# Four of eleven down tiles of each feed-forward as seven block products, moved behind the up tiles

## The reference

```python
def swiglu_ffn(x, w1, w2):
    a, b = jnp.split(x @ w1, 2, axis=-1)
    return (jax.nn.silu(a) * b) @ w2            # w1: 1024 x 5632, w2: 2816 x 1024

def conv_ffn(v, w_up, conv_w, conv_b, w_down):
    a, lin = jnp.split(v @ w_up, 2, axis=-1)
    a = sum(ap[:, j:j + s] * conv_w[j] for j in range(CONV_W)) + conv_b   # ap: a, padded; 3 taps
    return (jax.nn.gelu(a) * lin) @ w_down

# first block:   x = x + 0.5 * swiglu_ffn(rms_norm(x, g), w1, w2)    before and after the mixers
# second block:  x = x + conv_ffn(rms_norm(x, g), w_up, conv_w, conv_b, w_down)
```

## Time and profile before

| | us |
|---|---|
| median of 3 runs | 2239.8 (2239.71 to 2240.84) |
| the profiled execution | 2240.4 |
| its span, first to last instruction | 2238.7 |
| PE busy in the span | 2222.5 (99%) |
| DVE busy | 1529.8 (68%) |
| ACT busy | 1210.0 (54%) |
| DMA, bytes moved | 409.38 MB, mean 183 GB/s |

### The profile page before, as it was taken

How to read it: one execution, slowest core, us unless ns; L and a number is a source line. 1 busy time by engine, 2 the same in 40 slices (tenths; PEclk the granted TensorE clock), 3 DMA queues, 4 the chain that set the end, 5 groups by cost and what they waited for, 6 DMA issues and landing times.

```text
span 2238.7 us, 30449 instructions
## 1 busy us (share of the span) xinstructions
PE 2222.5 (99%) x12350; PEld 1898.8 (85%) x12350; DVE 1529.8 (68%) x2112; ACT 1210.0 (54%) x1812; POOL 67.6 (3%) x118
## 2 busy tenths in 40 slices
PE   8999999999999999999999999999999999999998
PEld 7888987888888889878888988888888988888887
DVE  6557578665665575786656866786777766786766
ACT  6456455454564564555545655455555555455554
POOL 0000000000000000000000200000000100000000
PEclk9999999999999999999999999999999999999999
DMA  8565544455545655434655544445555544445553
GB/s 286 192 232 184 199 180 151 171 188 188 188 186 190 232 186 204 182 144 169 232 189 190 187 151 165 156 153 181 190 192 178 189 151 165 156 166 181 188 188 113
DMA packets 62803, 409.38 MB, mean 183 GB/s; under 512 B 7976, under 2 KB 9512, under 8 KB 15304
## 3 DMA queue, kind: packets, MB, share of 16 engines
q1 hardware_dynamic: 62664, 407.44, 50.5%
HBM read 405.83 MB, written 2.10 MB: 182 GB/s over the span
## 4 chain that ended last, share of the span: by engine, by line
PE 94%; DVE 3%; ACT 1%; DMA 1%; issue 0%; SPq 0%; POOLq 0%; DVEq 0%; POOL 0%; ACTq 0%
PE bank L593 20%; PE bank L594 20%; PE bank L595 20%; PE bank L640 18%; PE bank L647 9%; DVE w_lo L270 1%; PE bank L393 1%; PE bank L1733 1%; PE bank L1745 1%; DMA w_raw<-in_tiles 0%; PE bank L2345 0%; PE bank L2052 0%; PE bank L2513 0%; PE bank L2062 0%; PE bank L2072 0%; PE bank L2532 0%
## 5 line engine op out<-in xcount | busy, mean ns | idle before, releaser
L270 DVE TENSOR_TENSOR w_lo<-w_raw,w_hi 128x2048 fp32r<-128x2048 f32 x367 | 835.1, 2284 | 69.0 <-ACT w_hi L240 68.6
L240 ACT ACTIVATE w_hi<-w_raw 128x2048 fp32r<-128x2048 f32 x359 | 685.3, 1912 | 107.7 <-DMA w_raw<-in_tiles 107.5
L640 PE MATMUL bank<-hT,w_hi 128*128 128x512 f32 x1920 | 459.5, 390 | 2.4 <-DVE w_lo L270 2.4
L640 PEld LDWEIGHTS bank<-hT,w_hi 128*128 128x128 f32 x1920 | 355.8, 188 | 73.8 <-DVE w_lo L270 2.8
L593 PE MATMUL bank<-w_hi,hT 128*128 128x512 f32 (+2 forms) x832 | 327.9, 394 | 0.3
L595 PE MATMUL bank<-w_hi,hT 128*128 128x512 f32 (+2 forms) x832 | 318.9, 383 | 0.0
L594 PE MATMUL bank<-w_lo,hT 128*128 128x512 f32 (+2 forms) x832 | 318.8, 383 | 0.0
L647 PEld LDWEIGHTS bank<-hT,w_lo 128*128 128x128 f32 x1920 | 247.7, 191 | 10.3
L647 PE MATMUL bank<-hT,w_lo 128*128 128x256 f32 x1920 | 250.9, 283 | 0.0
L593 PEld LDWEIGHTS bank<-w_hi,hT 128*128 128x128 f32 x832 | 156.8, 188 | 37.6 <-issue 7.9
L595 PEld LDWEIGHTS bank<-w_hi,hT 128*128 128x128 f32 x832 | 156.6, 188 | 31.3
(11 more groups left out here) (395 smaller groups left out, 2984.8 us busy)
## 6 DMA issues: line engine op xcount, KB each, us to landing
w_raw<-in_tiles SPq DMA_DIRECT2D x368, 1024.0 KB, 4.8
a_cmp_w<-in_cmp_w SPq DMA_DIRECT2D x2, 2048.0 KB, 7.8
shifted<-in_bias SPq DMA_DIRECT2D x12, 256.0 KB, 7.2
w_raw<-in_tiles SPq DMA_DIRECT2D x8, 256.0 KB, 5.7
a_gm_rows<-in_rows SPq DMA_DIRECT2D x2, 768.0 KB, 7.0
x_res<-in_x SPq DMA_DIRECT2D x2, 512.0 KB, 5.1
a_ret_rows<-in_rows SPq DMA_DIRECT2D x2, 512.0 KB, 8.0
b_rows<-in_rows SPq DMA_DIRECT2D x2, 512.0 KB, 6.2
```

The costliest lines, as they stand in the source:

```text
L240: act.activation(k.hi[slot][:], k.raw[slot][:], ACT.Copy).then_inc(k.hi_done[slot], 1)
L270: dve.tensor_tensor(k.lo[slot][:], k.raw[slot][:], k.hi[slot][:].bitcast(F32), ALU.subtract).then_inc(k.lo_done[slot], 1)
L640: pe.matmul(bank[:], k.hi[slot][:, w], k.hT[:, c].rearrange("p a s -> p (a s)"), start=c == 0, stop=False)
```

## The change

The feed-forwards' down tiles 2 to 8 move behind all up tiles. They then come in the order 2, 6, 3, 7, 4, 5, 8, before the two last, 9 and 10. Tiles 2, 3, 4, 5 (S) are multiplied by Strassen's algorithm in Winograd's form: the product of activations (2 x 2 blocks) and weights (2 x 2 blocks) takes seven block products in place of eight. DVE makes sums of weight blocks into a second, "made" tile that takes a ring slot of its own but is not loaded (`None` among the places); it is split into hi and lo as any other. DVE also makes four sums of activation blocks (`add_blocks`), which ACT and DVE split (`sums_hi`, `sums_lo`). Four of the products gather in banks 0 to 3, which the up tiles no longer need, and `recombine` adds them to x in eight steps. The activations of tiles 2 to 8 are kept in buffers of their own (`z_hi`, `z_lo`). Some semaphores are merged and some buffers moved to make room. A ring of 33 tiles becomes one of 37.

```diff
@@ class Ring
+    def make(self, dve, m, link):
+        k, slot, made = self.k, self.slot[m], self.slot[m + 1]
+        assert self.places[m + 1] is None and self.lo <= m
+        w = k.raw[slot][:].rearrange("p (c n e) -> p c n e", c=2, n=2)
+        t = k.raw[made][:].rearrange("p (q e) -> p q e", q=4)
+        dve.wait_ge(k.landed[slot], 16 * self.nth[m])
+        dve.wait_ge(k.used[made], self.before[m + 1])
+        link(dve.tensor_tensor(t[:, 0:2], w[:, :, 1], w[:, 0], ALU.subtract))
+        link(dve.tensor_tensor(t[:, 2], w[:, 1, 1], t[:, 0], ALU.subtract))
+        dve.tensor_tensor(t[:, 3], w[:, 1, 0], t[:, 2], ALU.subtract).then_inc(k.landed[made], 16)
...
+STRASSEN = (2, 3, 4, 5)
+LATER = (6, 7, 8)
+TAIL = (2, 6, 3, 7, 4, 5, 8)
+ENDING = (FFN_PAIRS - 2, FFN_PAIRS - 1)
+def ffn_order():
+    order = [("up", 0, 0), ("up", 0, 1)]
+    for i in range(1, FFN_PAIRS):
+        order += [("up", i, 0), ("up", i, 1)]
+        if i - 1 not in TAIL + ENDING:
+            order.append(("down", i - 1))
+    for i in TAIL + ENDING:
+        order.append(("down", i))
+        if i in STRASSEN:
+            order.append(("made", i))
+    return order
...
+    def strassen(self, pe, i):
...
+        ring.ready(pe, n)
+        product(self.acc[0][0], a12, n, 2, False, False)
+        product(self.acc[0][1], s4, n, 3, False, False)
+        if first:
+            for j in range(2):
+                pe.wait_ge(self.summed[j], self.parts(FFN_PAIRS - 1, 1))
+        product(k.bank[0], a11, n, 0, first, last).then_inc(k.used[ring.slot[n]], 1)
+        ring.ready(pe, n + 1)
+        product(self.acc[1][0], a22, n + 1, 3, False, False)
+        product(k.bank[1], s1, n + 1, 0, first, last)
+        product(k.bank[2], s2, n + 1, 2, first, last)
+        product(k.bank[3], s3, n + 1, 1, first, last).then_inc(k.used[ring.slot[n + 1]], 1)
@@ def tensor
-            if i < N - 1:
...
+            if i - 1 not in TAIL + ENDING:
+                self.whole(pe, i - 1)
+        pe.wait_ge(self.chain, self.links + 4 * len(STRASSEN))
+        for i in TAIL:
+            if i in STRASSEN:
+                self.strassen(pe, i)
+            else:
+                self.whole(pe, i)
@@ def scalar
                 self.split_hi(act, i, j)
+                if j == 0 and i - 1 in STRASSEN:
+                    self.sums_hi(act, i - 1)
             if i < FFN_PAIRS - 1:
                 k.ring.hi_to(act, self.up_at(i, 1) + SLOTS)
+        k.ring.hi_to(act, self.down_at(ENDING[0]) + 1)
+        k.ring.wait_used(act, self.down_at(STRASSEN[-1]) + 1, 1)
+        act.activation(self.flat(0), k.bank[0][:], ACT.Copy).then_inc(self.act_copy, 1)
+        k.ring.hi_to(act, self.end + 1)
@@ def vector
                 self.add_parts(dve, i, j, 1)
+                if j == 0 and i - 1 in STRASSEN:
+                    self.add_blocks(dve, i - 1, link)
                 self.combine(dve, i, j)
                 self.split_lo(dve, i, j)
+                if j == 1 and i - 1 in STRASSEN:
+                    self.sums_lo(dve, i - 1, link)
...
+            if i == FFN_PAIRS - 2:
+                ring.make(dve, self.down_at(STRASSEN[0]), link)
+            if i < FFN_PAIRS - 1:
                 ring.lo_to(dve, self.up_at(i, 1) + SLOTS - 1 + (self.conv is not None and i == 1))
+        for i in STRASSEN[1:]:
+            if i == STRASSEN[2]:
+                ring.lo_to(dve, self.down_at(i))
+            ring.make(dve, self.down_at(i), link)
+            ring.lo_to(dve, self.down_at(i) + 2)
+        ring.lo_to(dve, self.down_at(ENDING[0]) + 1)
+        self.recombine(dve, link)
+        ring.lo_to(dve, self.end)
...
+    def add_blocks(self, dve, i, link):
...
+        dve.tensor_tensor(s1, a21, a22, ALU.add)
+        link(dve.tensor_tensor(s3, a11, a21, ALU.subtract))
+        link(dve.tensor_tensor(s2, s1, a11, ALU.subtract))
+        link(dve.tensor_tensor(s4, a12, s2, ALU.subtract))
+    def sums_lo(self, dve, i, link):
+        n = STRASSEN.index(i)
+        dve.wait_ge(self.act_copy, self.act_copies + n + 1)
+        link(dve.tensor_tensor(self.z_lo[i][:, 3:7], self.sums[n % 2][:], self.z_hi[i][:, 3:7].bitcast(F32),
+                               ALU.subtract))
+    def recombine(self, dve, link):
...
+        k.ring.wait_used(dve, self.down_at(STRASSEN[-1]) + 1, 1)
+        dve.wait_ge(self.act_copy, self.act_copies + len(STRASSEN) + 1)
+        to_x(0, 0, p1)
+        link(dve.tensor_tensor(u, p6, u, ALU.add))
+        link(dve.tensor_tensor(v, p5, u, ALU.add))
+        to_x(0, 1, v)
+        link(dve.tensor_tensor(u, p7, u, ALU.add))
+        to_x(1, 0, u)
+        link(dve.tensor_tensor(v, p5, u, ALU.add))
+        link(to_x(1, 1, v))
```

More of the change, by code:

```diff
@@ L268, in lo_to @@
             slot = self.slot[m]
+            if m + 1 < len(self.places) and self.places[m + 1] is None:
+                dve.wait_ge(k.landed[self.slot[m + 1]], 16 * self.nth[m + 1])
             dve.wait_ge(k.hi_done[slot], self.nth[m])
@@ L648, in lo_part @@
     return last
-def ffn_places(base):
[L653 to L662, removed]
+STRASSEN = (2, 3, 4, 5)
[13 more added lines that the diff above has]
+    return order
+FFN_ORDER = ffn_order()
+FFN_AT = {tile: n for n, tile in enumerate(FFN_ORDER)}
+FFN_SIGNALS = [1 if tile[0] != "up" else 2 for tile in FFN_ORDER[:-1]] + [2]
+FFN_SIGNALS[0] = 1
+END_SIGNALS = FFN_SIGNALS[:-1] + [4]
+def ffn_places(base):
+    at = {"up": lambda i, j: base + 2 * i + j, "down": lambda i: base + 2 * FFN_PAIRS + i, "made": lambda i: None}
+    return [at[tile[0]](*tile[1:]) for tile in FFN_ORDER]
+LINKS = 6 * len(STRASSEN) + 5
 class Ffn:
@@ L752, in down, with activations, product @@
         return last
+    def activations(self, i, t, j):
+        if i in LATER:
+            return self.z_hi[i][:, 2 * j + t], self.z_lo[i][:, 2 * j + t]
+        ts = slice(t * P, (t + 1) * P)
+        return self.g_hi[i % 2][j][:, ts], self.g_lo[i % 2][j][:, ts]
+    def strassen(self, pe, i):
+        k, ring, n = self.k, self.k.ring, self.down_at(i)
+        a11, a12, a22, s1, s2, s3, s4 = range(7)
+        first, last = i == STRASSEN[0], i == STRASSEN[-1]
+        def product(bank, block, tile, q, start, stop):
+            w, slot = slice(q * 512, (q + 1) * 512), ring.slot[tile]
+            return three_passes(pe, bank[:], (self.z_hi[i][:, block], self.z_lo[i][:, block]),
+                                (k.hi[slot][:, w], k.lo[slot][:, w]), start, stop)
+        ring.ready(pe, n)
[10 more added lines that the diff above has]
+        product(k.bank[3], s3, n + 1, 1, first, last).then_inc(k.used[ring.slot[n + 1]], 1)
     def tensor(self, pe, following):
@@ L785, in tensor, with whole @@
                     last.then_inc(used(i), 1)
+    def whole(self, pe, i):
+        k = self.k
+        k.ring.ready(pe, self.down_at(i))
+        for j in range(2):
+            pe.wait_ge(self.glo_done[j], self.base + i + 1)
+            for t in range(NT):
+                last = self.down(pe, i, t, j)
+        last.then_inc(k.used[k.ring.slot[self.down_at(i)]], 1)
     def end_by_columns(self, pe, following):
@@ new lines, in vector @@
+        self.recombine(dve, link)
+        ring.lo_to(dve, self.end)
+        if self.block_end:
+            ring.lo_half(dve, self.end, 0)
+        else:
+            ring.lo_to(dve, self.end + 1)
+    def add_blocks(self, dve, i, link):
+        n = STRASSEN.index(i)
+        (a11, a21), (a12, a22) = ([g[:, t * P:(t + 1) * P] for t in range(NT)] for g in self.g)
+        s1, s2, s3, s4 = (self.sums[n % 2][:, q] for q in range(4))
+        for j in range(2):
+            dve.wait_ge(self.g_done[j], self.base + i + 1)
+        dve.tensor_tensor(s1, a21, a22, ALU.add)
+        link(dve.tensor_tensor(s3, a11, a21, ALU.subtract))
+        link(dve.tensor_tensor(s2, s1, a11, ALU.subtract))
+        link(dve.tensor_tensor(s4, a12, s2, ALU.subtract))
```

76 lines of the change are left out of this document (49 added, 27 removed).

## The result

The changed kernel takes 2328.85 us (median of four runs, 2326.01 to 2331.29), the kernel before beside it 2240.02 (2239.71 to 2240.84): a ratio of 1.0395, 95% interval 1.0383 to 1.0407, 88.8 us slower. The forecast was 2312 with a range of 2280 to 2335. The prediction was right in sign and range; the time lies 17 us above its value, 0.85 us above the upper end of the forecast itself (2300 to 2328), and in the stretch that the rival of the clock had (2316 to 2335). The profiled execution of the changed kernel spans 2329.5 us, that of before 2238.7.

The account below looks back on a forecast made before the run. PE, busy 99%, was taken as the bound, with VectorE's in-order list making it wait after the change. First block 16.7 us, second 57.0, about 1 off: +72.7, giving 2312 us; forecast 2300 to 2328, range 2280 to 2335.

Parts of the forecast that it names:

- the rival of the clock: Clock falls at new waits, above all the second block's 8 us one: +10 us, 2322; chance 0.10, most of it 2316-2335.
- PE's saving: A Strassen tile saves PE 0.68 us, a feed-forward with four of them 2.73, all six feed-forwards 16.4.
- VectorE's prices: VectorE's added work: making a tile 2.75 us, its split 2.20, block sums with low parts 1.95, recombining 5.45.
- Second block: Pairs of up tiles take VectorE 12.87 us, 14.8 with sums, against PE's 11.10; PE starts down tile 6 29.8 late.
- First block's turn: From up to down tiles, PE is 5.3 us late at tile 6: waits of 2.4 before a11, 2.9 before tile 6.
- Tile 10: End of the tail, both blocks: PE waits 1.4 us for its low part, 0.7 more once, ahead of the second block.
- The first block without the clock: First block's four feed-forwards together: 4 x (5.3 + 1.4 - 2.7) + 0.7 = 16.7 us slower.
- the prediction's own last sign: Forecast is wrong if PE's matmul steps of 0.43 us turn up behind the second block's long wait.
- the walk: Step-by-step count of VectorE's in-order list against PE's needs in all feed-forwards; it gave the forecast 2312 us, without the clock.
- The larger edit is the move: Moving tiles 2 to 8 behind the up tiles leaves VectorE 11.10 us per up pair, where it had 16.57.
- The rival in which the first block's turn costs nothing: Waits there are covered by slack in ACT or PE while the second block pays: +44 us, 2284; chance 0.12.
- The rival in which the saving stands: Second-block pairs pass through VectorE in 11.10 us or less, PE stays the bound: 2223.4 us; chance 0.06.

Follow-up runs that it names:

- order_fixed: The changed kernel with VectorE's list reordered at the turn in both blocks (first made tile earlier, down tile 6's low part before tile 3's making): 2303.69 us.
- zero_fill: The changed kernel with matmuls of a zero weight block put into PE's list where it waits in the tails: 2320.94 us.
- move_only: The changed kernel with the seven down tiles moved but all multiplied whole, without Strassen's work: 2259.2 us, ratio 1.0084 to the kernel before.
- first_block_only: The change in the first block's four feed-forwards only, the second block's two as in the kernel before: 2268.12 us, ratio 1.0125 to the kernel before.
- sums_on_gpsimd: The changed kernel with the activation block sums and their low parts on GpSimd in place of VectorE: 2319.89 us.

## Why the prediction was right, and where it was 17 us short

- **PE's saving**: as said. Two tiles in four feed-forwards gave 5.4 us where 5.5 were worked out.
- **VectorE's prices**: making a tile took 2.66 us (forecast 2.75), its instructions 1.22 and 0.69 as taken from rows of their sizes. The block sums and their low part made a pair 14.93 - 12.87 = 2.06 us longer (1.95). No unknown form surprised.
- **Second block**: pairs of 12.87 and 14.93 us (12.87 and 14.8); before tile 2 the wait was 2.73 (3), before a11 7.33 (8), up tile (3, 1) already waits as in the earlier trace rows. Per feed-forward 29.2 to 29.4 us without the clock; the forecast was 29.8 + 1.4 - 2.7 = 28.5. Tile 6 had no wait of its own: the 3 us went into the slow matmuls ahead of it.
- **First block's turn**: 2.27 and 2.50 to 2.55 us before a11 and tile 6, where 2.4 and 2.9 were said; no wait at its up tiles, as said. order_fixed shows the reason too.
- **Tile 10, mis-sized**: 1.4 us was said; it was 1.77 to 2.29 in three feed-forwards, 3.46 where 2.1 was said (feed-forward 4), and 2.06 and 1.96 in the second block. The recombining was priced well, but it starts late. VectorE's list ahead of it in feed-forward 2 of the change:

```profile
618.01 2.29 DVE L274 TENSOR_TENSOR w_lo<-w_raw,w_hi 128x2048 fp32r<-128x2048 f32 x1 [1.77 <-ACT w_hi L242]
620.77 2.29 DVE L274 TENSOR_TENSOR w_lo<-w_raw,w_hi 128x2048 fp32r<-128x2048 f32 x1 [0.47 <-ACT w_hi L242]
622.98 0.68 DVE L1040 SCALAR_TENSOR_TENSOR x_res<-bank,x_res 128x512 f32<-128x512 f32 x1
...
628.40 2.29 DVE L274 TENSOR_TENSOR w_lo<-w_raw,w_hi 128x2048 fp32r<-128x2048 f32 x1
```

 Recombining takes 628.40 - 622.98 = 5.42 us (5.45 was said). Counted from the end of tile 5's last product (620.78), tile 9's load is issued at -7.5, as worked out, but takes 5.5 us (613.32 to 618.79), not the median's 4.8, and 5.4 to 6.4 in the others. Why it takes longer no run here shows. Its low part ends at 2.2 in place of 1.7, recombining at 7.6 in place of 7.2, and PE starts tile 10 at 10.0 in place of 9.6. The wait of 1.77 us for tile 8 doesn't lengthen this path. In feed-forward 4 PE asks for tile 10 at 6.7, 1.5 us earlier than in feed-forward 2; 0.7 was said.
- **The first block without the clock**: in zero_fill its four feed-forwards come to 21.5 us against 16.7. In the change the idle time before a11 and tile 6 adds up to 19.2 us (21.2 said), that before tile 10 to 9.3 (6.3 said). The forecast put nothing on the edges of the waits; twelve waits at 0.23 to 0.25 us are some 3 us. These make 4 of the 4.8.
- **The clock, the term that was left out of the sum**: it was a rival with a tenth of the chance and +10 us, all in the second block behind the wait of 8 us, five for each of two tiles. It came, and cost 8 to 11 us, of which the second block has 2: the tile at 0.43 us a matmul stood in VectorE's shadow there. The rest fell in the first block, with waits of 1.8 to 3.5 us that the prediction hadn't asked about for the clock. The size came out near by luck; its place and reason did not. By the prediction's own last sign (matmul steps of 0.43 us behind the long wait) the forecast without the clock was wrong, and it was the range, made wide enough for this rival, that held the time. The Trainium skill, "TensorE: Matmul & The Clock Gate", section "Why this matters for your kernels", advises against idle gaps between bursts of matmuls; on this the trace agrees, and zero_fill puts the price on it.
- zero_fill parts the 17 us into 7.9 of the clock (2328.85 - 2320.94) and 8.9 of the walk (2320.94 - 2312). Of the 8.9 the table places 4.8 in the first block and 1.6 in the second (58.6 against 57.0). The rest isn't placed; the sum had taken off "about 1" for small savings and was rounded down by 0.5.
- "The larger edit is the move" fell with move_only: 18.9 us of 88.8.
- The rival in which the first block's turn costs nothing was out: in the change PE waits 4.8 us there in each feed-forward.
- The rival in which the saving stands was out for this change; with two tiles in the first block it is what happens.

What stays open: which of the waits of 1.8 to 2.6 us lower the clock. In the change the wait before a11 was 2.27 us in each of the first block's four feed-forwards and the matmuls behind it went on at full pace (in first_block_only the clock fell behind one of the four, in sums_on_gpsimd behind two), while it fell behind waits of 1.77 and 1.82 before tile 10. Nor is it the place: before tile 6 it fell behind 2.54 and 2.51 us (feed-forwards 1 and 4) and not behind 2.55 and 2.50 (2 and 3). No run here separates them.

## What to carry to other kernels

Before adding work to an engine that is 68% busy, walk its list in order from one wait of the bound engine to the next: the same instructions in another order were worth 25 us here. Take from a saving transformation only as much as the helping engine can prepare ahead: two of eleven tiles gave 5.4 us, a third gave nothing more, four in both blocks cost 89. A wait of PE of two microseconds can cost nearly twice itself: about 0.25 us at its edges, and 1.6 to 1.7 us if the clock falls, as it did with six of the first block's twelve. The second part costs nothing when another wait stands right behind it and hides the slow matmuls.

## What the runs showed of the hardware that I had not expected

- The granted clock fell to 0.50 behind waits as short as 1.77 us (feed-forward 3, before tile 10), stayed at 1.00 behind one of 2.55 us (feed-forward 2, before tile 6), and stayed at 1.00 behind every wait of up to 1.52 us looked at, also behind the second block's many waits of 0.7 to 1.4 us at its up tiles.
- Matmuls that do nothing but keep PE at work, 224 of them (51 us at full pace), made the kernel 7.9 us faster.
- A GpSimd subtraction of 128 columns took 0.46 us alone and 2.38 beside a split on VectorE, whose own 2.29 us became up to 2.95: of the 2.06 us of VectorE's work that left each pair, only 14.93 - 14.17 = 0.76 was won.
